# Four pages of a key/value cache share four places of a ring, each page on 32 partitions

## The reference, cut to what matters

```python
def one_seq(args):
    qi, ckv_i, kpe_i, pages = args
    ckv_all = jnp.concatenate([cache_ckv[pages].reshape(past, D_LATENT), ckv_i], axis=0)
    kpe_all = jnp.concatenate([cache_kpe[pages].reshape(past, D_ROPE), kpe_i], axis=0)
    k = mla_keys(ckv_all, kpe_all, w_uk, g_k)
    sc = jnp.einsum('qhd,khd->hqk', qi, k).astype(jnp.float32) * scale
    p = jax.nn.softmax(jnp.where(mask[None], sc, -jnp.inf), axis=-1)
    o_lat = jnp.einsum('hqk,kc->qhc', p, ckv_all)
```

## Time and profile before

| | us |
|---|---|
| median of 3 runs (2628.03 to 2641.3) | 2634.8 |
| the profiled execution | 2627.88 |
| its span from first to last instruction | 2626.2 |
| DVE busy in the span | 2156.1 |
| PE busy | 2201.2 |
| from 1230 to 2350 us (the pages' stage), time | 1120 |

### The profile page before, as it was taken

The page is one execution under the profiler, slowest core; times in us unless marked ns, Lnnn a source line. Parts: engine busy times, 40 slices in busy tenths (PEclk is TensorE's granted clock), DMA queues, the critical chain, the costliest instruction groups (busy, mean ns, idle before and its releaser), DMA issues.

```text
span 2626.2 us, 36376 instructions
## 1 busy us (share of the span) xinstructions
PE 2201.2 (84%) x11497; PEld 1571.4 (60%) x11497; DVE 2156.1 (82%) x4009; ACT 917.3 (35%) x3596; POOL 1353.3 (52%) x1209
## 2 busy tenths in 40 slices
PE   5999998997989988687999999999999889963232
PEld 3999998884448854344665656565656556642020
DVE  3775688995555326988999999999999989999797
ACT  3331101333252003213445454555454545441110
POOL 0221231112002103776777777777777777777574
PEclk8999999998999999798999999999999989985666
DMA  6334877455007767999999999999999999999997
GB/s 207 98 85 128 217 216 195 130 157 158 13 16 221 217 203 263 388 396 400 403 396 381 406 384 404 374 402 375 401 366 399 382 392 408 363 406 396 400 403 276
DMA packets 385726, 776.49 MB, mean 296 GB/s; under 512 B 50473, under 2 KB 200058, under 8 KB 385497
## 3 DMA queue, kind: packets, MB, share of 16 engines
q0 software_dynamic: 154704, 562.94, 55.6%
q1 hardware_dynamic: 209498, 186.53, 23.0%
q10 hardware_dynamic: 21332, 24.70, 2.9%
HBM read 744.85 MB, written 29.37 MB: 295 GB/s over the span
## 4 chain that ended last, share of the span: by engine, by line
DVE 25%; issue 15%; DMA 12%; PE 6%; POOL 4%; ACT 1%; SPq 0%; DVEq 0%; POOLq 0%; ACTq 0%
DVE mix_pair L2655 11%; DVE mix_u L2754 9%; DMA mix_u<-in_peer_u,mix_ids 7%; DMA chs_wq<-in_peer_wq 3%; PE mix_pair L2199 2%; POOL mix_v L2157 2%; POOL mix_u L2150 2%; PE mix_pair L2256 2%; PE mix_pair L2167 1%; DMA pag_kpe<-in_cache_kpe 1%; DMA keep_x<-mix_sc 1%; DMA mix_v<-in_peer_v,mix_ids_half 1%; PE mix_pair L2276 0%; DMA mix_u<-in_peer_u,mix_ids_half 0%; DVE mix_s L1829 0%
## 5 line engine op out<-in xcount | busy, mean ns | idle before, releaser
L2256 PE MATMUL mix_pair<-pag_wx,pag_ckvT 128*128 128x384 f32 (+3 forms) x3072 | 945.4, 462 | 17.4 <-ACT mix_pair L2466 12.3
L2256 PEld LDWEIGHTS mix_pair<-pag_wx,pag_ckvT 128*128 128x128 f32 x3072 | 579.8, 194 | 314.9 <-issue 23.3
L2157 POOL DMA_INDIRECT mix_v<-in_peer_v,mix_ids x512 | 618.2, 1207 | 182.4 <-issue 169.9
L2150 POOL DMA_INDIRECT mix_u<-in_peer_u,mix_ids x512 | 550.0, 1074 | 268.2 <-issue 145.3
L2754 DVE CUSTOM_DVE_ANT_0 mix_u<-mix_u,mix_h 128x1024 f32<-128x1024 f32 x512 | 621.6, 1214 | 52.4 <-DMA mix_u<-in_peer_u,mix_ids 50.7
L2655 DVE SCALAR_TENSOR_TENSOR mix_pair<-mix_v,mix_coef,mix_pair 128x1024 f32<-128x1024 f32 x508 | 650.4, 1280 | 1.3 <-DMA mix_v<-in_peer_v,mix_ids 1.3
L2466 ACT ACTIVATE mix_pair<-mix_pair 128x128 f32<-128x128 f32 x1024 | 269.2, 263 | 316.7 <-PE mix_pair L2256 316.5
L373 PE MATMUL inp_ps<-inp_h_hi,inp_w_hi 128*128 128x260 f32 x1168 | 340.1, 291 | 21.5 <-DVE inp_w_lo L367 14.4
L375 PE MATMUL inp_ps<-inp_h_hi,inp_w_lo 128*128 128x260 f32 x1168 | 333.7, 286 | 0.0
L374 PE MATMUL inp_ps<-inp_h_lo,inp_w_hi 128*128 128x260 f32 x1168 | 333.3, 285 | 0.0
L407 POOL CAST inp_w_hi<-inp_w 128x1024 fp32r<-128x1024 f32 x73 | 88.8, 1216 | 374.7 <-DMA inp_w<-in_w_in 314.6
(11 more groups left out here) (540 smaller groups left out, 3209.8 us busy)
## 6 DMA issues: line engine op xcount, KB each, us to landing
inp_w<-in_w_in SPq DMA_DIRECT2D x72, 512.0 KB, 4.6
pag_ckv<-in_cache_ckv SPq DMA_DIRECT2D x80, 256.0 KB, 16.6
mrg_w_ada<-in_w_ada SPq DMA_DIRECT2D x16, 1024.0 KB, 8.5
all_shared<-in_cache_ckv SPq DMA_DIRECT2D x48, 256.0 KB, 17.0
chs_wq<-in_peer_wq SPq DMA_DIRECT2D x11, 1024.0 KB, 20.1
keep_proj<-stp_out ACTq DMA_DIRECT2D x32, 260.0 KB, 3.8
stp_st<-in_state_ssm POOLq DMA_DIRECT2D x8, 1024.0 KB, 7.5
out_ssm_s<-stp_st POOLq DMA_DIRECT2D x8, 1024.0 KB, 6.7
```

The lines of the kernel that those rows point to most:

```text
L2150: pool.indirect_dma_start(u[:, x % UR, :], None, u_rows, bass.IndirectOffsetOnAxis(at, 0)).then_inc(u_in[x % UR], 16)
L2157: pool.indirect_dma_start(v[:, y % VR, :], None, v_rows, bass.IndirectOffsetOnAxis(at, 0)).then_inc(v_in[y % VR], 16)
L2256: last = pe.matmul(to, ckvT[:, g % 2, k, :], wx[:, k, lo:hi], start=(k == 0), stop=(k == KL - 1))
```

## The change

`load_page` puts page g on the 32 partitions that begin at 32 * (g % 4), and there across the four places of its group of four: partition 32 * (g % 4) + i gets tokens 4i to 4i + 3 of the page, one in each place. A place then holds 32 tokens of each of four pages. As the four places are one behind the other in a partition's memory, what a partition reads for a page is one contiguous run of 4 x 2048 bytes for the latents and 4 x 256 bytes for the rotary part, on both sides. The semaphores, their counts, the transfers' number and the order on SP stay: the transfers on SP become 32x2048 and 32x256 numbers where they were 128x512 and 128x64. No instruction of another engine is added, removed or moved.

```diff
+TOGETHER = 4
...
+        page_group = lambda r: (ckv[:, r:r + TOGETHER, :] if r < NPG - SHARED else ckv_shared[:, r - (NPG - SHARED):r - (NPG - SHARED) + TOGETHER, :]).rearrange("p r c -> p (r c)")
+        rope_group = lambda g: o_raw[:, g * ROPE:(g + TOGETHER) * ROPE] if g < SHARED else kpe[:, ring(g):ring(g) + TOGETHER, :].rearrange("p r c -> p (r c)")
...
             def load_page(g):
                 page = sp.value_load(table[0:1, g:g + 1], min_val=0, max_val=A["cache_ckv"].shape[1] - 1)
-                sp.dma_start(page_rows(ring(g)), A["cache_ckv"][0, bass.ds(page, 1)].rearrange("a p c -> (a p) c")).then_inc(page_in[ring(g) // 4], 16)
-                sp.dma_start(rope_rows(g), A["cache_kpe"][0, bass.ds(page, 1)].rearrange("a p c -> (a p) c")).then_inc(page_in[ring(g) // 4], 16)
+                first, at = g - g % TOGETHER, slice(g % TOGETHER * PAGE // TOGETHER, (g % TOGETHER + 1) * PAGE // TOGETHER)
+                sp.dma_start(page_group(ring(first))[at, :], A["cache_ckv"][0, bass.ds(page, 1)].rearrange("a (p n) c -> (a p) (n c)", n=TOGETHER)).then_inc(page_in[ring(g) // 4], 16)
+                sp.dma_start(rope_group(first)[at, :], A["cache_kpe"][0, bass.ds(page, 1)].rearrange("a (p n) c -> (a p) (n c)", n=TOGETHER)).then_inc(page_in[ring(g) // 4], 16)
```

## The result

The changed kernel takes 2771.12 us in the median of 4 runs (2766.18 to 2779.51), the kernel before 2635.37; the ratio is 1.0525, with a 95% interval of 1.0497 to 1.0552. The forecast was 2720 with a range of 2640 to 2770: right in direction and in mechanism, too small by 51 us, and the median lies 1 us outside the range. The profiled execution took 2779.51 us with a span of 2777.7, 151.5 us over the one before.

What follows compares the result with a forecast made beforehand. DVE was taken to set the pace with DMA nearly full; 2627.88 + 90 for slower page bursts + 5 for pages 0 to 23 gave 2723 us, stated as 2720, range 2640 to 2770.

Steps and rivals of the forecast that it cites:

- What bounds the kernel: From 1050 us on, DVE sets the pace; DMA, at 387 to 402 GB/s, has little room above DVE's demand.
- Packets: Page loads: data packets per page fall from 256 to 64, saving 14 us of DMA time for 128 pages.
- Turns: Queues sharing DMA engines packet for packet: pages take 53% of what the engines move, where they took 22%.
- Partitions: Page writes on 32 partitions have half of the way in, 213 against 406 GB/s, and hold up the other queue.
- Rate in a burst: DMA during a group of 16 pages: 278 GB/s in all, between bounds of 243 and 400.
- The mixed row: Earlier trace of POOL's loads on 64 partitions beside SP's on 128: 243 GB/s together, taken as lower bound in a burst.
- Lead: Gathers' 6 and 7 buffers hide 3.1 us per burst, leaving DVE waiting 17.0 us where it waited 3.1.
- Rival 2: Gather buffers in bursts: lead is deeper, 8.7 us hidden; no change, 2630 us; chance 11%.
- Pages 0 to 23: Early page loads, before the bursts: +5 us in all, about half of the paced pages' cost covered by DMA's room.
- rival 4: Page bursts: way in no limit, shorter bursts and saved DMA time remove DVE's waits, at most 21.7 us; 2608; 9%.
- Rival 1: Page bursts: only packet turns matter, the mix stays at 400 GB/s; +23 us, 2651; chance 14%.
- Rival 3: Page bursts, worst case: 243 GB/s, +120 and +10 us, 2758; far end of the main forecast, 66% together.

Runs made afterwards that it cites:

- every4_3: Changed kernel with each page on every fourth partition instead of 32 neighbours, packets still 8192 and 1024 bytes; 2631.03 us, 0.9991 to the kernel before.
- small_3: Changed kernel with pages still on 32 neighbouring partitions but packets back at 2048 and 256 bytes; 2768.62 us, 1.0524 to the kernel before.

## Why the prediction was wrong in size

*What bounds the kernel* held: DVE sets the pace and DMA has next to no room. The whole loss is DVE's wait for `u`, as said, and it was not given back. The step that failed is a size, the rate in a burst: 278 GB/s was taken, and 254 down to 226 measured. Beside it the +5 us for pages 0 to 23 were 26.5.

*Packets.* The 24,576 packets fewer are there, and what they save is worth nothing that can be measured: `every4_3` keeps the saving without the loss and has 0.9991 (0.9975 to 1.0007), with 68.6 us of waits for `u` against 50.7.

*Turns.* Mis-sized: "pages take 53% of what the engines move". The packets that count the semaphores take turns too; they are in the count of 1698 to 1701 from which the rule was read the earlier trace rows, but I left them out of the mean size after. With them a page is 96 packets of 3072 bytes on the mean against the gathers' 3640, 46%; measured 3.25 of 7.08 MB, 46%.

*Partitions.* Held, and shown by `small_3` and `every4_3`.

*Rate in a burst.* This is the step that failed: "I take 278". Measured 254 in the first group, and 226 from 1930 to 1950 us in a later one:

```profile
DMA packets 1348, 4.53 MB, mean 226 GB/s; under 512 B 301, under 2 KB 527, under 8 KB 1122
```

Six stretches of 15 us in the second, third and fifth group have 238 to 255. The mixed row, 243 GB/s, was the better guide; 278 came from dividing the sustained 213 by a share, as if the half were used without a gap while packets of two queues meet at it. That there are such gaps is my reading, and no run separates it. With its own 53% and 278 the sum had 20.1 us of lack in a group; with 108 and 128 GB/s as measured, a group lasts 4.72 MB / 108 = 43.7 us (q1's packets are seen for some 47 us from 1441 us on, where 32 were forecast), the gathers lack 220 x 43.7 = 9.6 MB, 9.2 slots, 27.7 us.

*Lead.* Mis-sized the other way: of these 27.7 us DVE waited 17.9 in the first group, so the buffers hid 9.8 us and not 3.1. Rival 2 was right in that. In the first group the two errors cancel, 17.9 us waited against the forecast's 17.0, and that is luck. Over all groups they don't: +13.9 us a group was forecast, +20 measured as the mean (149.9 less 21.6 over 6.5), +90 against +128 in all. It is the later groups, with 20 to 29 us, that take the sum up. The lower rate is one part of that (226 from 1930 to 1950 us, where the group waited 23.2), but not all: the sixth group has 248 GB/s from 2255 to 2270 us and the longest waits, 28.8. Why was not tested.

*Pages 0 to 23.* "+5 in all" was 26.5 by the trace. I let the room of 58 GB/s cover half of the paced pages' cost, but DMA had been at 402 GB/s all through that window with DVE at 139.86 of 140, and that was the row to go by: next to no room. Pages 8 to 12 are issued behind each other from 1238 to 1248 us besides, a small burst.

*Sum.* 90 and 5 were 128.3 and 26.5: 154.8 of the 156.8 us. The sum for the profiled execution was 2723, and the median lay 7 us above it, so 2730 and not 2720 followed; rival 4's 2627.88 less 21.7 is 2606 and not 2608. Neither matters here. A shorter way would have been nearer, with the 46% of *Turns*: a page at 243 GB/s with its share of the gathers, 294.9 KB / 0.46 = 641 KB, takes 2.64 us and at 400 1.60; 1.04 us more for each of 128 pages is 133 us, if nothing hides it.

*PE* did not gain, as forecast: its wait for pages went from 26.9 to 21.0 us, and it now waits more for ACT (66.6 us at `mix_pair`, 12.3 before).

*Rivals.* Rival 1 and rival 4, a mix that stays near 400 GB/s, fell with 254 GB/s in the changed kernel; both describe `every4_3`, which keeps the packets and does stay there, and neither rival's +23 nor -20 us came even then. Rival 3, at 243 GB/s, was the nearest with 2758.

## What to carry to other kernels

Where DMA is full, price a transfer by the time of the engines that it takes, summed over all of them, and not by how a burst fits the buffers: spreading it gave back a quarter, packet size nothing. Lay a tile of 32 partitions on every fourth partition and not on neighbours; with the same packets the gathers and pages together moved 412 or 254 GB/s. And where DMA's share is 1.0 with fewer GB/s than in the next window, take the time of one packet: 236 ns for the 148 of the same gather before was the sign of crowded writes. Small packets lower the GB/s too, 396 for 406, but in the kernel before they left a gather's packet at 148 ns, where it takes 146 alone.

## What the runs showed of the hardware that was not expected

Two queues that both have packets waiting share an engine packet for packet, and a packet that only counts a semaphore takes a turn like one of 8192 bytes: the counts agree (1052 to 1055, 2398 to 2398) only with these in them. Writes on 32 neighbours slow the other queue's packets as well, 148 to 236 ns for a gather's. 64 neighbouring partitions are no better than 32 (277 to 308 GB/s against 254 and 308). A penalty of 5.1% on one chip was 1.9% on another whose kernel before took 2823 us; a ratio measured on such a chip is not the same quantity.
